# A two-layer encoder step on one core: when pairs of hidden tiles are split, and who adds the last output tiles

## The reference

```python
def swiglu(x, w_gate, w_up, w_down):
    a = jnp.einsum('btd,df->btf', x, w_gate)
    b = jnp.einsum('btd,df->btf', x, w_up)
    return jnp.einsum('btf,fd->btd', jax.nn.silu(a) * b, w_down)      # d = 1024, f = 2816
...
ff_a = swiglu(rms_norm(x, g[0]), ...)
x = x + 0.5 * rms_norm(ff_a, g[1])
h = rms_norm(x, g[2]); x = x + rms_norm(mix(h), g[3])     # latent + band attention, or grouped window attention
ff_b = swiglu(rms_norm(x, g[4]), ...)
x = x + 0.5 * rms_norm(ff_b, g[5])
```

## Time and profile before

| | before |
|---|---|
| median of three runs | 1947.75 us (1947.28 to 1948.30) |
| the profiled execution | 1948.25 us, its span 1946.4 us |
| TensorE busy | 1894.0 us, 97% of the span, 15600 matmuls |
| VectorE, ScalarE, GpSimd busy | 78%, 57%, 22% |
| granted TensorE clock, mean | 0.993 |
| chain that ended last | TensorE 76%, VectorE 12%, GpSimd 4%, ScalarE 4% |

### The profile page before, as it was taken

The page is one execution under the profiler, slowest core; times in us unless marked ns, Lnnn a source line. Parts: engine busy times, 40 slices in busy tenths (PEclk is TensorE's granted clock), DMA queues, the critical chain, the costliest instruction groups (busy, mean ns, idle before and its releaser), DMA issues.

```text
span 1946.4 us, 38781 instructions
## 1 busy us (share of the span) xinstructions
PE 1894.0 (97%) x15600; PEld 1834.5 (94%) x15600; DVE 1522.2 (78%) x1996; ACT 1114.9 (57%) x2133; POOL 419.2 (22%) x413
## 2 busy tenths in 40 slices
PE   9999999999999999999999999999999999999997
PEld 9999999999669999999999999999997999999997
DVE  7889897774773888989868789897767487898976
ACT  7565566431684655565655655656438556556562
POOL 0013130300352101323020013130336200131302
PEclk9999999999999999999999999999999999999999
DMA  4322222332311222323232223233231222232322
GB/s 162 104 83 93 103 94 98 98 104 77 122 45 44 66 87 87 109 87 98 93 104 66 98 83 113 82 111 96 92 111 54 69 73 98 82 114 82 101 99 70
DMA packets 59025, 177.95 MB, mean 91 GB/s; under 512 B 7056, under 2 KB 11488, under 8 KB 58720
## 3 DMA queue, kind: packets, MB, share of 16 engines
q1 hardware_dynamic: 56720, 167.66, 26.0%
q0 software_dynamic: 2128, 7.80, 1.3%
HBM read 168.26 MB, written 5.36 MB: 89 GB/s over the span
## 4 chain that ended last, share of the span: by engine, by line
PE 76%; DVE 12%; POOL 4%; ACT 4%; issue 4%; DMA 0%; DVEq 0%; ACTq 0%; POOLq 0%; SPq 0%
PE psum L826 23%; PE psum L828 23%; PE psum L827 23%; DVE w_lo L726 4%; ACT w_hi L723 2%; POOL fold_raw L2595 2%; DVE h_raw L2204 2%; DVE h_lo L2212 2%; POOL h_raw L2597 1%; PE psum L1156 1%; DVE fold_lo L2218 1%; PE psum L1142 1%; DVE y L2001 1%; PE psum L1275 1%; DVE xlo L2099 1%
## 5 line engine op out<-in xcount | busy, mean ns | idle before, releaser
L826 PE MATMUL psum<-xhi,w_hi 128*128 128x272 f32 x1632 | 478.8, 293 | 15.5 <-DVE w_lo L726 14.3
L828 PE MATMUL psum<-xhi,w_lo 128*128 128x272 f32 x1632 | 473.0, 290 | 0.0
L827 PE MATMUL psum<-xlo,w_hi 128*128 128x272 f32 x1632 | 471.7, 289 | 0.0
L826 PEld LDWEIGHTS psum<-xhi,w_hi 128*128 128x128 f32 x1632 | 310.0, 190 | 22.6 <-DVE w_lo L726 17.8
L726 DVE TENSOR_TENSOR w_lo<-w_raw,w_hi 128x1024 fp32r<-128x1024 f32 (+1 forms) x208 | 236.7, 1138 | 118.0 <-ACT w_hi L723 116.3
L827 PEld LDWEIGHTS psum<-xlo,w_hi 128*128 128x128 f32 x1632 | 309.9, 190 | 0.7
L828 PEld LDWEIGHTS psum<-xhi,w_lo 128*128 128x128 f32 x1632 | 309.0, 189 | 0.0
L828 PE MATMUL psum<-corner,w_lo 128*128 128x272 f32 x864 | 249.9, 289 | 0.0
L827 PE MATMUL psum<-corner,w_hi 128*128 128x272 f32 x864 | 249.5, 289 | 0.0
L826 PE MATMUL psum<-corner,w_hi 128*128 128x272 f32 x864 | 248.6, 288 | 0.0
L826 PE MATMUL psum<-h_hi,w_hi 128*128 128x272 f32 x832 | 240.2, 289 | 0.9
(11 more groups left out here) (327 smaller groups left out, 4760.3 us busy)
## 6 DMA issues: line engine op xcount, KB each, us to landing
w_raw<-in_w_gate_up SPq DMA_DIRECT2D x172, 512.0 KB, 4.1
w_raw<-in_w_down SPq DMA_DIRECT2D x96, 384.0 KB, 3.5
w_raw<-in_w_down SPq DMA_DIRECT2D x32, 256.0 KB, 2.7
w_raw<-in_even_in SPq DMA_DIRECT2D x16, 512.0 KB, 3.3
w_raw<-in_odd_in SPq DMA_DIRECT2D x10, 512.0 KB, 3.9
w_raw<-in_even_out SPq DMA_DIRECT2D x8, 512.0 KB, 3.8
w_raw<-in_odd_out SPq DMA_DIRECT2D x8, 512.0 KB, 4.0
out_band_kv<-qkvb POOLq DMA_DIRECT2D x1, 2176.0 KB, 10.0
```

The source lines that it names most:

```text
L826: nc.tensor.matmul(out, s_hi, m_hi, start=first, stop=False, skip_group_check=skip)
L827: nc.tensor.matmul(out, s_hi, m_lo, start=False, stop=False, skip_group_check=skip)
L828: return nc.tensor.matmul(out, s_lo, m_hi, start=False, stop=last, skip_group_check=skip)
```

## The change

Five things. (1) The splits of pairs 0, 1, 3 and 4 (`pair_high`, `fold_high`, `pair_low`, `fold_low`) move from the step that multiplies the pair to the step after it; product and GpSimd's sums stay. (2) For pairs 2 and 5, behind which a fold step comes, they stay in their step, but ScalarE's `pair_high` moves behind `copy_corner` and split 0. (3) In the first fold steps TensorE waits for one pair at a time. (4) The last four tiles of the last pass (i = 12 to 15) are not added by VectorE: ScalarE copies y into the bank (`put`) and the matmuls add on top; ScalarE then squares the bank and copies it to y, scaled by the gain. (5) In consequence `last_update` takes these tiles in pairs with one plain product; `post_sum` and `post_last` of H = 1 go behind tiles 3 and 5 of the unit; ScalarE's results 12 and 13 come ahead of the roundings of x tiles 5 and 7.

```diff
+ADDED = 12
+PUT = 2 * KD - ADDED
...
+def made_pair(k):
+    kind, j = STEPS[k]
+    return j // 2 - 1 if kind == "seven" and j % 2 == 0 and j > 0 else None
+def split_pair(k):
+    made = made_pair(k)
+    if made in (2, 5) or made is not None and made >= FOLDED:
+        return made
+    before = made_pair(k - 1) if k > 0 and STEPS[k][0] == STEPS[k - 1][0] == "seven" else None
+    return before if before is not None and before < FOLDED and before not in (2, 5) else None
...
@@ first_steps (TensorE)
-                    mids = {(1, 0): lambda: post_sum(s - 1, 1), (1, 2): lambda: post_last(s - 1, 1)}
+                    mids = {(1, 3): lambda: post_sum(s - 1, 1), (1, 5): lambda: post_last(s - 1, 1)}
...
-                    pe.wait_ge(y_whole, 2 * KD * (ffn_no(s) - 1) + 14)
+                    pe.wait_ge(y_scaled, PUT * (ffn_no(s) - 1) + 2)
                 in_half(s, g + 1, 0, 4)
...
@@ step (TensorE): the waits on fold_low_done and pair_lo move into the loop over t
+                        if kind == "fold" and j % 4 == 0:
+                            if name in ("T1", "T2", "B22"):
+                                pe.wait_ge(fold_low_done, FOLDED * n + 3 * (j // 4) + t + 1)
+                            else:
+                                pe.wait_ge(pair_lo, len(PAIRS) * n + 3 * (j // 4) + t + 1)
...
@@ last_tiles, last_pass (TensorE)
-                             k == 0, k == PASS - 1)
+                             k == 0 and i < ADDED, k == PASS - 1, i >= ADDED)
...
-                    pe.wait_ge(y_whole, 2 * KD * n + i - 3)
+                    if i < ADDED:
+                        pe.wait_ge(y_whole, ADDED * n + i - 3)
+                    else:
+                        pe.wait_ge(y_put, PUT * n + i - ADDED + 1)
...
@@ after_last_pass (ScalarE), without the splits
+                for i in (8, 9):
+                    last_result(s, i)
+                    put(s, i + 4)
                 post_std(c, 0)
...
-                    if k in (1, 3, 5):
+                    if k in (1, 3):
                         last_result(s, 10 + k // 2)
-                for i in range(13, 2 * KD):
+                        put(s, 14 + k // 2)
+                    elif k in (4, 6):
+                        last_result(s, 10 + k // 2)
+                for i in (14, 15):
                     last_result(s, i)
...
@@ last_result (ScalarE), for i >= ADDED
+                whole = psum[:, LAST_BANKS[i % 4], 0:TH]
+                nc.scalar.activation(scratch[:, m % 4, :], whole, ACT.Square).then_inc(ysq_ready, 1)
+                nc.scalar.activation(y[:, m, HALF[H]], whole, ACT.Copy,
+                                     scale=post_gains[:, s, m:m + 1]).then_inc(y_scaled, 1)
+            def put(s, i):
+                m, H = OUT_ORDER[i]
+                act.wait_ge(y_whole, ADDED * ffn_no(s) + i - 3)
+                nc.scalar.activation(psum[:, LAST_BANKS[i % 4], 0:TH], y[:, m, HALF[H]], ACT.Copy).then_inc(y_put, 1)
...
@@ the loop over STEPS (ScalarE)
-                    seven, made = kind == "seven", j // 2 - 1 if kind == "seven" and j % 2 == 0 and j > 0 else None
+                    seven, made = kind == "seven", split_pair(k)
...
-                    if made is not None:
+                    late = made in (2, 5)
+                    if made is not None and not late:
                         pair_high(s, made)
...
+                    if late:
+                        pair_high(s, made)
                     keep(s, k, "T3")
...
@@ last_update, after_last_pass (VectorE)
+                    if OUT_ORDER.index((2 * j, H)) >= ADDED:
+                        dve.wait_ge(y_scaled, PUT * (ffn_no(s) + 1) - KD + 2 * j + 2)
+                        two = y[:, 2 * j:2 * j + 2, HALF[H]]
+                        return own(nc.vector.tensor_tensor(two, two, twice, ALU.mult))
...
-                last_update(c, 0, {j: lambda i=10 + j: add_last(s, i) for j in range(3)})
-                add_last(s, 13)
-                add_last(s, 14)
+                last_update(c, 0, {j: lambda i=10 + j: add_last(s, i) for j in range(2)})
...
-                add_last(s, 15)
...
@@ the loop over STEPS (VectorE)
-                    if made is not None:
-                        pair_low(s, made)
-                        if made < FOLDED:
-                            fold_low(s, made)
+                    if low is not None:
+                        pair_low(s, low)
+                        if low < FOLDED:
+                            fold_low(s, low)
```

More of the change, by code:

```diff
@@ L426, in build @@
         y_whole = sem("y_whole")
+        y_put = sem("y_put")
+        y_scaled = sem("y_scaled")
         y_ready = sem("y_ready")
@@ L901, in first_steps @@
                     pe.wait_ge(ysq_ready, 16 * s)
+                if after_ffn(s):
+                    pe.wait_ge(y_scaled, PUT * ffn_no(s))
                 if s > 0:
@@ L919, in step @@
                         pe.wait_ge(part_lo_done, 7 * n + i + 1)
[L920 to L924, removed]
                     if name not in ("B11", "T1"):
@@ L1597, in after_last_pass @@
             def after_last_pass(c):
[L1599 to L1609, removed]
+                s, g, more = c - 1, G0[c], c < len(SUBS)
+                if more:
+                    split_unit(act, "act", g, 0)
+                for i in (8, 9):
+                    last_result(s, i)
+                    put(s, i + 4)
                 post_std(c, 0)
-                split_unit(act, "act", g, 1)
+                if more:
+                    split_unit(act, "act", g, 1)
                 for k in range(KD):
-                    act.wait_ge(x_ready, 16 * s + k + 1)
-                    high_part(c, 0, k)
-                    if k in (1, 3, 5):
+                    if more:
+                        act.wait_ge(x_ready, 16 * s + k + 1)
+                        high_part(c, 0, k)
+                    if k in (1, 3):
                         last_result(s, 10 + k // 2)
-                for i in range(13, 2 * KD):
+                        put(s, 14 + k // 2)
+                    elif k in (4, 6):
+                        last_result(s, 10 + k // 2)
+                for i in (14, 15):
                     last_result(s, i)
-                    if i < 15:
-                        for k in range(4 * (i - 13), 4 * (i - 13) + 4):
+                    if more:
+                        for k in range(4 * (i - 14), 4 * (i - 14) + 4):
                             square(c, 0, k)
-                split_unit(act, "act", g + 1, 0)
+                if more:
+                    split_unit(act, "act", g + 1, 0)
             def boundary(c):
@@ L1715, in last_result @@
                 m, H = OUT_ORDER[i]
-                act.wait_ge(y_whole, 2 * KD * ffn_no(s) + i + 1)
+                if i < ADDED:
+                    act.wait_ge(y_whole, ADDED * ffn_no(s) + i + 1)
+                else:
+                    act.wait_ge(y_ready, y_event(s, m, H) + 1)
                 if i >= 4:
                     act.wait_ge(ysq_summed, total_event(s, *OUT_ORDER[i - 4]) + 1)
-                nc.scalar.activation(scratch[:, m % 4, :], y[:, m, HALF[H]], ACT.Square).then_inc(ysq_ready, 1)
+                if i < ADDED:
+                    nc.scalar.activation(scratch[:, m % 4, :], y[:, m, HALF[H]], ACT.Square).then_inc(ysq_ready, 1)
+                    return
+                whole = psum[:, LAST_BANKS[i % 4], 0:TH]
[6 more added lines that the diff above has]
+                nc.scalar.activation(psum[:, LAST_BANKS[i % 4], 0:TH], y[:, m, HALF[H]], ACT.Copy).then_inc(y_put, 1)
             def keep(s, k, name):
@@ L1996, in last_update @@
                 s = c - 1
+                r = rstd[:, HALF[H]]
+                twice = bass.AP(r.tensor, r.offset, [r.ap[0], [0, 2], r.ap[1]])
                 def scaled(j):
+                    if OUT_ORDER.index((2 * j, H)) >= ADDED:
+                        dve.wait_ge(y_scaled, PUT * (ffn_no(s) + 1) - KD + 2 * j + 2)
+                        two = y[:, 2 * j:2 * j + 2, HALF[H]]
+                        return own(nc.vector.tensor_tensor(two, two, twice, ALU.mult))
                     for m in (2 * j, 2 * j + 1):
@@ L2251, in ffn_dve @@
                 for k, (kind, j) in enumerate(STEPS):
-                    made = j // 2 - 1 if kind == "seven" and j % 2 == 0 and j > 0 else None
+                    made, low = made_pair(k), split_pair(k)
                     if k > 0:
@@ L2624, in ffn_pool @@
                         sum_fold(s, k)
-                    elif j % 2 == 0 and 0 < j // 2 <= FOLDED:
-                        fold_sums(s, j // 2 - 1)
+                    elif made_pair(k) is not None and made_pair(k) < FOLDED:
+                        fold_sums(s, made_pair(k))
                 sum_y(s)
```

3 lines of the change are left out of this document (1 added, 2 removed).

## The result

The changed kernel takes **1925.26 us**, median of four runs (1923.76 to 1926.86), against 1948.03 (1947.28 to 1949.05) for the kernel before on the same chip: the ratio is 0.9883, 95% interval 0.9866 to 0.9900. That is 22.8 us less. The forecast was 39.2 less, and its range ended at 1923: the sign was right, the size was not, and the time lies outside the range.

What follows compares the result with a forecast made beforehand. TensorE, 97% busy, bounds the kernel, so only its stalls or slow stretches can be won. 26 + 1.5 + 10.5 + 1.2 = 39.2 us off 1948.25 gives 1909.0, median 1908.5; range 1899 to 1923.

Steps and rivals of the forecast that it cites:

- Pairs 2 and 5: Steps of these pairs and first fold steps, 8 times: gain 0.2 each, 1.5 us in all, at most 7.
- The lateness: VectorE leaves the preceding step late, so the next pair's product starts 4.3 us behind T4 in place of 2.65.
- `pair_low` goes at 9.3: Step of pair 2: pair_high ends at 9.2 behind T4, pair_low follows at 9.3, and T1 starts at 12.5.
- rival 3: Pairs 1 and 4: VectorE's weight sums wait out GpSimd on the shared port; 8 us lost, 1917; chance 0.04.
- Pairs 0, 1, 3, 4: Losses ahead of T4 and the next T1 go, about 0.1 remains: gain 1.6 each, 16 make 26 us.
- The ends: Ends of FFNs 0, 2 and 3: post_sum's stall and the lower clock go; 10.5 us for three.
- g's loss of 0.41: FFN end, group g at 383.10: its split needs VectorE at 381.1, so the 0.41 goes.
- a new stall: FFN ends: TensorE stands still for 1.7 us waiting for the split of g + 1.
- The last end: Last FFN's end: 0.8 of post_sum's wait goes, two plain products save 0.2 each; 1.2 us, between 0.4 and 1.7.
- Rival 1: Most FFN ends: the clock falls at the new wait of 1.7, costing 1.3 to 2.5 each; 1914; chance 0.16.
- Slower, or no change: VectorE bounds the pair's two steps, 1953, chance 0.03; or pair waits and end stalls merely move, 1947, chance 0.03.
- rival 2: Pair steps: VectorE's lateness isn't made up, the 0.3 margin fails; 0.7 at 16 pairs, 11 us, 1920; chance 0.14.

Runs made afterwards that it cites:

- Experiment 3: Also called early_lows: the changed kernel with later-step pair operations moved earlier in that step, VectorE's low parts ahead of split 0; 1910.94 us, ratio 0.9807.
- experiment 4: The changed kernel with GpSimd's second addition of pair 5 over 16 columns in place of 272; 1921.62 us in one run.
- copies_behind: The changed kernel with ScalarE's scaled copies of tiles 14 and 15 behind the squares and the split of g + 1; 1922.68 us, ratio 0.9858.
- post_later: The kernel before with only post_sum and post_last of H = 1 three tiles later; 1945.01 us over ten runs, ratio 0.9986.

## Why the prediction was right or wrong

**Pairs 2 and 5: a gain of 1.5 forecast, a loss of 7.4 measured; 8.9 of the 16.4 that are missing lie here.** The lateness was forecast well (product at 4.25 for 4.3; T4 loses 0.35 for 0.5), though the terms that the forecast lists for it add up to 4.6: the last, 0.57, already holds the second addition. The step that failed is "`pair_low` goes at 9.3": I let it start with the end of `pair_high` and didn't follow its second wait, on GpSimd's fourth addition (`fold_made` at 4). Before, that addition was done 1.15 ahead of `pair_low`; with the product 1.6 later it is not. It ends at 10.6 behind T4, `pair_low` starts at 10.7, and the 1.3 to 1.4 go straight into T1 (13.8 for 12.5). Of the 1.3 by which the addition passes 9.3, 0.7 was to be had from the kernel before (4.25 + 5.77 = 10.0), and 0.6 is the collision with split 0. Experiment 3 takes the lateness away and the loss with it, and experiment 4 moves the addition, `pair_low` and T1 together, though VectorE's own queue with them.

**The shared port: rival 3 was right in its mechanism and wrong in its place.** I had read a sum of 1.15 in place of 0.69 as a slower instruction. The new rows say otherwise, and so did a row of the kernel before that I hadn't set beside it:

```profile
107.58 1.10 POOL L2597 TENSOR_TENSOR h_raw<-h_raw 128x272 f32<-128x272 f32 x1
```

This addition ends at 108.68; 0.69 behind that is 109.37, and the sum's row ends at 109.24. In the changed kernel split 0 starts at 152.70 inside an addition that ends at 153.42 and ends at 154.23, within 0.15 of that end plus its own 0.95. The next addition starts at 153.50 inside the split, and ends 0.64 behind it. Whoever comes second waits out the first, and its row's duration holds the waiting. The Trainium skill states that the second is blocked until the first is done (SBUF — State Buffer, "SBUF: two separate sides"); the trace agrees for these two-operand instructions. That the row's duration holds the waiting is what the rows here show. The place was not the step of pairs 1 and 4, where I had put it: there two splits last 1.79 and 1.80 in place of 1.22 (at 131.68 and 133.40 in the trace after) and TensorE loses 0.2 there, where the rival had 1.0. It was the fold step, where both engines are on one chain, and where I had used no such term.

**Pairs 0, 1, 3, 4: 22.8 for 26.** The 1.73 goes as forecast. By starts pair 0 wins 1.74 and pair 1 only 1.50, since VectorE's two lengthened splits leave its T1 0.2 late; then each gives back 0.2 at the next T1, for the 0.1 forecast. 1.74 + 1.50 - 0.4 = 2.84 for two pairs. I had priced all 16 by the first one.

**The ends: 8.2 for 10.5.** Mechanism right: no wait in `post_sum`, the puts hidden, the clock at 1.00, a new stall of 1.6 for the 1.7 forecast, and low parts of H = 1 that cost 0.70 and 0.48 for 0.7 and 0.5. Mis-sized is g's loss of 0.41, which I took to go and which became 0.79 by two collisions with GpSimd: 0.8 at each of three ends is the whole of the missing 2.3. The stall of 1.6 is partly luck. `sum_x` starts at 381.07 where the forecast gives 384.3 - 4.0 = 380.3 (4.0 were won before), and the split of g + 1 is 0.7 late with it; TensorE comes 0.8 late itself, and the two cancel. The last end gave 1.06 for 1.2.

**The clock.** Rival 1 didn't come: behind six idle times of up to 1.44 at the ends the clock stayed at 1.00. But it fell once where I hadn't looked, in the attention of the first mixer:

```profile
509.54 0.88 PE L1143 MATMUL psum<-kN,qN 64*64 64x64 f32 x16 [1.44 <-ACT probsE L1496]
```
```profile
510.30:515.30 5.00, 5.00 (x40) 1.93 (x38) 1.36 (x4) 2.64 (x12) 2.82 (x2) 0.66 0.01 3
```

The same idle time stood there before (1.43), and 58 matmuls went in the same work at 1.00. In 6 of the 14 profiled executions (one for each kernel) the clock fell there and in 8 it didn't, with an idle time of 1.43 or 1.44 in every one. It cost 1.6 in this run. In that of copies_behind the clock stood at 0.50 from 509.1 to 529.4, which cost 7.7 more. What decides it stays open.

**Slower, or no change:** neither came. Of the rivals' prices rival 2's 11 us is nearest to the shortfall of 16.4, but its mechanism didn't come: the two steps of 22.87 shrank to 21.12, those of pair 1 to 21.56.

## What to carry to other kernels

Follow every semaphore of an instruction that you move, to the count it waits for: one that was always long met becomes the bound once its producer comes late. When work moves later, look for what it newly lies beside on VectorE and GpSimd and count the neighbour's full duration, and put it where its engine is idle ahead of the critical instruction: the same instructions a few places earlier in their queues gave 14 us more.

## What the runs showed of the hardware

- VectorE and GpSimd wait each other out: 1.53 for 0.95 and 1.37 for 0.78 in one chain of encounters, where each came second to the other's instruction; in early_lows the first comer kept its 0.96 and the second took 1.49. The waiting lies inside the row's duration, so a blocked instruction reads like a slow one.
- An idle time of TensorE of 2.02 to 2.04 was followed by a granted clock of 0.72 over the next 6 us at two ends of post_later and by 1.00 at the third; 1.44 at the ends was followed by 1.00, and 1.43 to 1.44 in the mixer by a fall in 6 of 14 executions. Idle time alone doesn't tell these apart.
- ScalarE's square of 272 columns took 0.38 to 0.41 out of PSUM and 0.41 to 0.43 out of SBUF. A value that it puts into PSUM is taken up by the matmuls that add to it, at no cost to TensorE: through the last pass of the first FFN the difference of starts stays at -4.02.
